# Scores of the first attention on four quarters of the array, fused sum and extreme, and the delta rule's joins as 32x32 products

## The chip, the cores and the metric

The kernel runs on one core of a Trainium2 chip. The metric is the device time of one execution in microseconds (us). The core has a matrix engine (TensorE, PE in the profile, with its weight loads as PEld), VectorE (DVE), ScalarE (ACT), GpSimd (POOL) and a queue that issues transfers (SyncE, SP). Each engine works through its own list of instructions in order; they wait for one another by semaphores.

## What is computed

Two blocks of a model on 1024 tokens of width 1024, in float32. The change touches two places.

In the first block, neighbourhood attention: 8 heads of size 64, tokens as 16 rows of 64. A row of queries sees the keys of 8 rows (512 keys), with a bias and a mask.

```python
scores = jnp.einsum('bhrnqd,bhrnikd->bhrnqik', q_blk, kg).astype(jnp.float32)
scores = jnp.where(valid[:, :, None, :], scores + bias[None], -1e30)
probs = jax.nn.softmax(scores, axis=(-2, -1)).astype(v.dtype)
out = jnp.einsum('bhrnqik,bhrnikd->bhrnqd', probs, vg)
```

In the second block, a gated delta rule in both directions over 1280 tokens in chunks of 64. Each chunk needs the inverse of a lower triangular matrix for each of 8 heads:

```python
t_mat = jnp.eye(CHUNK, dtype=jnp.float32) + bc[..., :, None] * dec_strict * kk
w_mat = lax.linalg.triangular_solve(t_mat, (bc * eG)[..., None] * kc, left_side=True, lower=True, unit_diagonal=True)
```

## The kernel before, in words

Each engine's list is written out by hand, one function for each stage and engine. PSUM's eight banks are drawn in turn by an object `bk`: `open(key)` takes the next bank, `vacant(key)` is the wait for the one who emptied it eight draws ago, `full` and `clear` are filled and emptied.

**First attention** (`tensor_natt`, `vector_natt`, `scalar_natt`, `gpsimd_natt`). The work is 64 units: unit i is one row r = i // 4 of 64 queries with a pair of heads j = i % 4. The two heads are laid out as 128 rows of a score tile of 512 keys. The queries lie in `QB` with zeros in the other head's half (cleared by two memsets, L559), so that one product of full size (contraction 128, 128 rows, 512 columns; L591) gives both heads. In PE's list iteration i holds the scores of unit i, the four transposes of unit i-3 (L600) and the eight value products of unit i-4 (L617, each on 64 columns of the array). A float32 product is two records of the profile, a transpose one. DVE adds the bias into one of two buffers `sb` (L632), takes the negated maximum (L636) and the reciprocal of the sum (L641), and splits the finished values in two (L647, L649). ACT makes the exponential with its sum (L659), then copies the transposed tile out of PSUM for unit i-3 (L667). GpSimd scales the exponentials by the reciprocal (L674) ahead of the transposes.

After the last unit the recurrent part follows (`tensor_rec`, its products under L95).

**Queries** (`vector_query_out`, L512): DVE writes each 128x512 result into `QB` in two instructions of 64 partitions.

**Delta rule** (`tensor_delta` and the others). A step takes one 128-token tile in each direction (dd = 0, 1), ten steps n. Blocks of 32x32 on the diagonal are inverted on DVE by elimination (L2241, L2244), go out to DRAM and come back in two layouts, `Y0` and `YT`; the joins then build 64x64 inverses from pairs of 32x32 ones, and 128x128 ones from those:

- join a (L2286): 16 products with a full `AT` (128x128) and `Y0` (64 columns); ACT copies four blocks of 32 partitions (L2298) into `PM`, whose other places are zero.
- join b (L2309): 16 products of full `PM` with `YT`; ACT copies four blocks back into `YT` (L2317).
- joins c, d, e (L2330, L2348, L2366): 64x64 products, with a copy by ACT after each.
- Between them stand the decay rows (L95 here) and the next key products (L2153).
- Then the step uses the inverse (L2410), DVE scales that result (L2418) in the midst of its next elimination, and so on: L2436, L2445, L2458 and L2388 on PE.

The transfers of `YT` are issued by SP (L2275), and join b waits for them (`l_yt`).

## Time and profile before

| | |
|---|---|
| Median of 3 runs | 3741.59 us (3739.25 to 3743.46) |
| The profiled execution | 3733.37 us, span 3731.6 us |
| PE busy | 3562.2 us, 95% |
| DVE, ACT, POOL busy | 1847.5, 1186.6, 704.0 us |
| Mean granted clock of TensorE | 0.981 |
| First attention, PE from its first score to the next stage | 165.1 to 322.1 us |
| Delta rule, joins a of the first and last step | 1937.7 and 2287.1 us |

Times are from the start of the span. A group of the profile gives busy time and mean length; an idle time names what ended it. Lengths of records on PE contain some 0.2 us of pipeline, so the pace of PE is read from the starts, not from the lengths.

### The profile page before, as it was taken

Reading aid. Unit: us, or ns where it says so; the run is one execution under the profiler, and the core shown is the slowest. Engines: PE = TensorE matmul, PEld = TensorE weight load, DVE = VectorE, ACT = ScalarE, POOL = GpSimd, SP = SyncE. Lnnn points to the kernel's source line nnn. Section 1 sums busy time; section 2 is a strip of 40 time slices with the busy share of each in tenths; the row PEclk is TensorE's granted clock in tenths of the full one; section 3 lists DMA queues with packets and bytes.
Section 4 is the critical chain, followed back from the end, with each engine's and each line's share of the span. In section 5 each row is a group of like instructions: output and inputs, shape, how many; then the busy total and the mean of one; then the engine's idle time right before and its main releaser. Section 6 shows DMA issues by size and latency. Waiting matters only on the chain. (4 is left out here: it accounts for less than half of the span.)

```text
span 3731.6 us, 46421 instructions
## 1 busy us (share of the span) xinstructions
PE 3562.2 (95%) x18318; PEld 2764.2 (74%) x18318; DVE 1847.5 (50%) x3351; ACT 1186.6 (32%) x2087; POOL 704.0 (19%) x532
## 2 busy tenths in 40 slices
PE   7999999999999999999988988988999999999998
PEld 6756778887888888875557877546788478888886
DVE  4276993213676555335578884669211142322322
ACT  3155772212311111234434553138211032111210
POOL 1163000010101111010020110129101113333333
PEclk9999999999999999999999998999999999999999
DMA  3100111112233232123012214000122111111111
GB/s 134 37 2 22 44 40 51 54 55 87 75 106 96 91 105 93 46 78 125 1 22 41 39 38 138 27 1 2 35 74 59 54 57 46 51 51 46 49 53 46
DMA packets 266342, 211.67 MB, mean 57 GB/s; under 512 B 65680, under 2 KB 231184, under 8 KB 265744
## 3 DMA queue, kind: packets, MB, share of 16 engines
q1 hardware_dynamic: 264368, 201.61, 17.4%
q10 hardware_dynamic: 1760, 7.08, 0.9%
q8 instruction: 149, 2.44, 0.3%
q14 instruction: 65, 0.53, 0.0%
HBM read 185.33 MB, written 21.50 MB: 55 GB/s over the span
## 5 line engine op out<-in xcount | busy, mean ns | idle before, releaser
L95 PE MATMUL ps<-halves 128*128 128x512 f32 x10408 | 2406.7, 392 | 19.1 <-DVE halves L1542 6.6
L95 PEld LDWEIGHTS ps<-halves 128*128 128x128 f32 x10408 | 1956.1, 188 | 441.4 <-issue 26.9
L95 PE MATMUL ps<-arena 128*128 128x512 f32 (+1 forms) x880 | 361.7, 564 | 11.2 <-issue 6.4
L1521 POOL TENSOR_TENSOR tmps<-tmps 128x512 f32<-128x512 f32 x128 | 143.7, 1123 | 981.4 <-ACT tmps L1489 981.4
L1542 DVE TENSOR_TENSOR halves<-tmps,halves 128x512 fp32r<-128x512 f32 x128 | 88.1, 691 | 435.4 <-ACT halves L1497 435.4
L1425 ACT ACTIVATE halves<-raws 128x2048 fp32r<-128x2048 f32 x62 | 118.3, 1909 | 556.0 <-PE ps L95 532.5
L95 PEld LDWEIGHTS ps<-arena 128*128 128x128 f32 x880 | 165.7, 193 | 170.3 <-issue 159.3
L1528 POOL TENSOR_TENSOR arena<-arena 128x512 f32<-128x512 f32 x128 | 164.8, 1294 | 191.3 <-DVE arena L1569 191.3
L1489 ACT ACTIVATE tmps<-ps 128x512 f32<-128x512 f32 x128 | 76.6, 598 | 363.9 <-PE ps L95 360.0
L1569 DVE TENSOR_TENSOR arena<-ps,arena 128x512 f32<-128x512 f32 x128 | 87.8, 690 | 194.9 <-PE ps L95 188.7
L1365 DVE SCALAR_TENSOR_TENSOR arena<-arena,sc 128x128 f32<-128x128 f32 x448 | 164.1, 366 | 15.9
L1432 DVE TENSOR_TENSOR halves<-raws,halves 128x2048 fp32r<-128x2048 f32 x62 | 142.0, 2290 | 55.3 <-ACT halves L1425 55.3
L95 PE MATMUL ps<-arena,tokens 128*128 128x512 f32 (+1 forms) x384 | 140.2, 523 | 0.0
L2943 POOL TENSOR_SCALAR arena<-arena,wst 128x640 f32<-128x640 f32 (+1 forms) x64 | 119.0, 1873 | 89.8 <-DVE wst L2897 89.7
L1559 DVE TENSOR_TENSOR arena<-arena,ps 128x512 f32<-128x512 f32 x128 | 85.2, 683 | 99.7 <-PE ps L95 99.7
L674 POOL TENSOR_SCALAR arena<-arena,sm 128x512 f32<-128x512 f32 x64 | 100.1, 1565 | 176.1 <-DVE sm L641 176.1
L2116 POOL TENSOR_TENSOR arena<-arena 128x512 f32<-128x512 f32 x40 | 44.5, 1140 | 455.0 <-PE ps L95 232.5
L1497 ACT ACTIVATE halves<-tmps 128x512 fp32r<-128x512 f32 x128 | 81.0, 633 | 154.5 <-POOL tmps L1521 154.5
L95 PEld LDWEIGHTS ps<-arena,tokens 128*128 128x128 f32 x384 | 72.4, 191 | 62.2 <-issue 59.2
L2244 DVE TENSOR_TENSOR arena<-arena 64x30 f32<-64x30 f32 (+5 forms) x300 | 103.9, 346 | 10.3
L2241 DVE TENSOR_TENSOR arena<-arena 64x30 f32<-64x30 f32 (+5 forms) x300 | 102.9, 343 | 10.0
L1093 POOL TENSOR_TENSOR valw<-valw,arena 128x512 f32<-128x512 f32 x8 | 14.0, 1748 | 444.3 <-DVE arena L1076 444.3
(306 smaller groups left out, 3532.3 us busy)
## 6 DMA issues: line engine op xcount, KB each, us to landing
raws<-in_w_ff SPq DMA_DIRECT2D x31, 1024.0 KB, 6.5
raws<-in_w_mlp SPq DMA_DIRECT2D x31, 1024.0 KB, 5.4
mixw<-in_w_in SPq DMA_DIRECT2D x56, 512.0 KB, 3.8
arena<-in_w_ada SPq DMA_DIRECT2D x48, 512.0 KB, 3.9
arena<-in_w_in SPq DMA_DIRECT2D x5, 2048.0 KB, 11.9
arena<-in_x SPq DMA_DIRECT2D x8, 1024.0 KB, 8.3
h_stash<-arena SPq DMA_DIRECT2D x1, 5120.0 KB, 30.0
inverses<-arena ACTq DMA_DIRECT2D x20, 256.0 KB, 2.9
```

What stands on the lines that cost most here:

```text
L95: ins = e.matmul(out_ap, l, r, start=i == 0, stop=i == n - 1)
L674: e.tensor_scalar(pbuf[i % 5], pbuf[i % 5], c[:, 2:3], None, ALU.mult).then_inc(*a_sl.tick())
L1365: e.scalar_tensor_tensor(out=a, in0=raw_a[:, kk, :], scalar=sc3[:, kk, b:b + 1], in1=a, op0=ALU.mult, op1=ALU.add).then_inc(*(m_part if kk ...
L1425: e.activation(RR[:, FW + q * 4096:FW + q * 4096 + 2048], raw_of(n), ACT.Copy).then_inc(*f_wh.tick())
L1432: e.tensor_tensor(RR[:, FW + q * 4096 + 2048:FW + q * 4096 + 4096], raw_of(n), RR[:, FW + q * 4096:FW + q * 4096 + 2048].bitcast(F32), ALU ...
L1521: e.tensor_tensor(tt, tt, tt, ALU.mult).then_inc(*f_sq.tick())
L1528: e.tensor_tensor(dst, dst, tmg[(i * 8 + t) % 2], ALU.add).then_inc(*f_ad.tick())
L1542: e.tensor_tensor(fl[:, m, n0:n0 + N], ftmp[x % 2], fh[:, m, n0:n0 + N].bitcast(F32), ALU.subtract).then_inc(*f_fl.tick())
L1569: e.tensor_tensor(tmg[x % 2], bk.tile(key)[:, :], G2[:, nh * 512:nh * 512 + 512], ALU.mult).then_inc(*bk.emptying(key))
L2241: e.tensor_tensor(T3, bc(W3[:, k:k + 1, k + 1:32], [64, k, 31 - k]), bc(W3[:, 0:k, k:k + 1], [64, k, 31 - k]), ALU.mult).then_inc(*dv.tick())
L2244: e.tensor_tensor(W3[:, 0:k, k + 1:32], W3[:, 0:k, k + 1:32], T3, ALU.add).then_inc(*(i_sol if k == 30 else dv).tick())
L2943: ins = e.tensor_scalar(p, p, w4[i % 4][:, 6 + s:7 + s], None, ALU.mult)
```

## The change

Three parts.

**Scores.** `QB`'s other half is no longer used and no longer cleared. A unit's two heads are two products of contraction 64 and 64 rows, each on a quarter of the array. `natt_rows(i, s)` puts head s of unit i into rows 0 to 63 or 64 to 127, exchanged in odd units; the host exchanges the bias the same way. Scores are issued for two units at once, so that four products that follow one another lie on the four quarters. Values are taken one unit later (i-5). DVE's sum and maximum become one instruction, `tensor_tensor_reduce`, which writes the negated sum and its minimum; ACT's exponential takes scale -1. The order on DVE changes, with the reciprocals in pairs.

**Queries.** One instruction of 128 partitions instead of two of 64.

**Joins a and b.** Both directions share one bank and one key. Each head's product is four 32x32 products, on four places of the array that share neither rows nor columns. `PM` and `Y0` are 256 columns, their memsets go, and ACT's four copies after join a become one of 128x256. After join b there are still four.

```diff
-            e.wait_ge(*q_zero.at(m // 2 + 1))
+            e.wait_ge(*n_xn.at(8))
             e.wait_ge(*bk.full(key))
-            for s in range(2):
-                rows = slice(64 * s, 64 * s + 64)
-                ins = e.tensor_scalar(
-                    QB[rows, m, 8 * h:8 * h + 8, s, :],
-                    bk.tile(key)[rows, :].rearrange("p (r q) -> p r q", q=64), V("bq", m)[rows], 0.125,
-                    ALU.add, ALU.mult)
-            ins.then_inc(*bk.emptying(key))
+            e.tensor_scalar(QB[:, m, 8 * h:8 * h + 8, 0, :], bk.tile(key)[:, :].rearrange("p (r q) -> p r q", q=64),
+                            V("bq", m), 0.125, ALU.add, ALU.mult).then_inc(*bk.emptying(key))
...
-            for i in range(2):
-                e.wait_ge(*n_xn.at(4 * i + 4))
-                e.memset(R(F0 + 4096 * i, 4096), 0.0).then_inc(*q_zero.tick())
...
+        def natt_rows(i, s):
+
+            a = 64 * ((s + i) % 2)
+            return slice(a, a + 64)
+
         def tensor_natt(e):
-            for i in range(64 + 4):
-                if i < 64:
-                    r, j, start = natt_place(i)
-                    key = ("as", i)
-                    o = bk.open(key, a_ev)
-                    e.wait_ge(*bk.vacant(key))
+            for i in range(64 + 5):
+                if i < 64 and i % 2 == 0:
+                    for u in (i, i + 1):
+                        bk.open(("as", u), a_es)
+                        e.wait_ge(*bk.vacant(("as", u)))
                     if i == 0:
                         e.wait_ge(*bk.clear(("q", 3, 1)))
                         e.wait_ge(*bk.clear(("k", 3, 1)))
-                    e.matmul(o[:, :], QB[:, j, r, :, :], KT[:, j, start * 64:start * 64 + 512], start=True,
-                             stop=True).then_inc(*bk.filling(key))
+                    for s in range(2):
+                        for u in (i, i + 1):
+                            r, j, start = natt_place(u)
+                            f = slice(64 * s, 64 * s + 64)
+                            ins = e.matmul(bk.tile(("as", u))[natt_rows(u, s), :], QB[f, j, r, 0, :],
+                                           KT[f, j, start * 64:start * 64 + 512], start=True, stop=True)
+                            if s == 1:
+                                ins.then_inc(*bk.filling(("as", u)))
...
-                if 0 <= i - 4 < 64:
-                    u = i - 4
+                if 0 <= i - 5 < 64:
+                    u = i - 5
...
-                                           ptb[u % 3][:, c, f], start=c == 0, stop=c == 3)
+                                           ptb[u % 3][:, c, natt_rows(u, s)], start=c == 0, stop=c == 3)
...
-                    e.tensor_tensor(sb[i % 2], bk.tile(key)[:, :], BI[:, j, off * 64:off * 64 + 512],
-                                    ALU.add).then_inc(*bk.emptying(key))
-                    c = statn[:, i % 8, :]
-                    e.wait_ge(*bk.clear(key))
-                    e.tensor_reduce(c[:, 0:1], sb[i % 2], AX.X, ALU.max, negate=True).then_inc(*a_mx.tick())
-                u = i - 1
-                if 0 <= u < 64:
-                    c = statn[:, u % 8, :]
-                    e.wait_ge(*a_ex.at(u + 1))
-                    e.reciprocal(c[:, 2:3], c[:, 1:2]).then_inc(*a_rc.tick())
-                if 0 <= i - 4 < 64:
-                    u = i - 4
-                    r, j, start = natt_place(u)
-                    key = ("ap", u)
-                    e.wait_ge(*bk.full(key))
-                    e.tensor_copy(YAH[:, j, r, :], bk.tile(key)[:, 0:64]).then_inc(*dv.tick())
-                    e.wait_ge(*dv.now())
-                    e.tensor_tensor(YAL[:, j, r, :], bk.tile(key)[:, 0:64], YAH[:, j, r, :].bitcast(F32),
-                                    ALU.subtract).then_inc(*bk.emptying(key))
+                    e.tensor_tensor_reduce(out=sb[i % 2], in0=bk.tile(key)[:, :], in1=BI[:, j, off * 64:off * 64 + 512],
+                                           scale=-1.0, scalar=3.0e38, op0=ALU.add, op1=ALU.min,
+                                           accum_out=statn[:, i % 8, 0:1]).then_inc(*bk.emptying(key))
+                for u in ((), (i - 1, i))[i % 2]:
+                    if u < 64:
+                        c = statn[:, u % 8, :]
+                        if u == i and i >= 5:
+                            vector_natt_out(e, i - 5)
+                        e.wait_ge(*a_ex.at(u + 1))
+                        e.reciprocal(c[:, 2:3], c[:, 1:2]).then_inc(*a_rc.tick())
+                if i >= 5 and (i % 2 == 0 or i >= 64):
+                    vector_natt_out(e, i - 5)
+
+        def vector_natt_out(e, u):
+            r, j, start = natt_place(u)
+            key = ("ap", u)
+            e.wait_ge(*bk.full(key))
+            e.tensor_copy(YAH[:, j, r, :], bk.tile(key)[:, 0:64]).then_inc(*dv.tick())
+            e.wait_ge(*dv.now())
+            e.tensor_tensor(YAL[:, j, r, :], bk.tile(key)[:, 0:64], YAH[:, j, r, :].bitcast(F32),
+                            ALU.subtract).then_inc(*bk.emptying(key))
...
-                    e.wait_ge(*a_mx.at(i + 1))
+                    e.wait_ge(*bk.clear(("as", i)))
                     if i >= 5:
                         e.wait_ge(*bk.full(("at", i - 5)))
-                    e.activation(pbuf[i % 5], sb[i % 2], ACT.Exp, bias=c[:, 0:1],
+                    e.activation(pbuf[i % 5], sb[i % 2], ACT.Exp, bias=c[:, 0:1], scale=-1.0,
...
-        PM = [M4(16384 + i * 1024) for i in range(2)]
-        Y0 = [R3(18432 + i * 512, 8, 64) for i in range(2)]
+        PM, Y0 = R3(16384, 8, 32), R3(18432, 8, 32)
+        QUARTERS = [(dd, q) for q in range(2) for dd in range(2)]
...
-        def tensor_join_a(e, n, dd):
-            key = ("la", n, dd)
+        def tensor_join_a(e, n):
+
+            key = ("la", n)
             o = bk.open(key, e_ea)
             e.wait_ge(*bk.vacant(key))
             e.wait_ge(*l_y0.at(4 * (n + 1)))
-            e.wait_ge(*bk.clear(("kk", n, dd, 1)))
+            for dd in range(2):
+                e.wait_ge(*bk.clear(("kk", n, dd, 1)))
             for h in range(8):
-                ins = e.matmul(o[:, h * 64:h * 64 + 64], AT[n % 2][dd][:, h, :], Y0[dd][:, h, :], start=True, stop=True)
+                for dd, q in QUARTERS:
+                    first, second = blk32(FIRST(dd, q)), blk32(SECOND(dd, q))
+                    ins = e.matmul(o[second, h * 32:h * 32 + 32], AT[n % 2][dd][first, h, second], Y0[first, h, :],
+                                   start=True, stop=True)
             ins.then_inc(*bk.filling(key))
 
-        def scalar_join_a(e, n, dd):
-            key = ("la", n, dd)
+        def scalar_join_a(e, n):
+            key = ("la", n)
             e.wait_ge(*bk.full(key))
             if n:
-                e.wait_ge(*bk.full(("lt", n - 1, dd)))
-            else:
-                e.wait_ge(*s_zero.at(3))
-            for q in range(2):
-                r = blk32(SECOND(dd, q))
-                ins = e.activation(PM[dd][r, :, blk32(FIRST(dd, q))], h8(bk.tile(key))[r, :, blk32(q)], ACT.Copy)
-            ins.then_inc(*bk.emptying(key))
-
-        def tensor_join_b(e, n, dd):
-            key = ("lt", n, dd)
+                e.wait_ge(*bk.full(("lt", n - 1)))
+            e.activation(PM, q8(bk.tile(key)), ACT.Copy).then_inc(*bk.emptying(key))
+
+        def tensor_join_b(e, n):
+            key = ("lt", n)
             o = bk.open(key, e_ea)
             e.wait_ge(*bk.vacant(key))
-            e.wait_ge(*bk.clear(("la", n, dd)))
+            e.wait_ge(*bk.clear(("la", n)))
             e.wait_ge(*l_yt.at(8 * (n + 1)))
-            y = YT[n % 2][dd].rearrange("p h (q s f) -> p h q s f", q=2, s=2)
             for h in range(8):
-                ins = e.matmul(o[:, h * 64:h * 64 + 64], PM[dd][:, h, :], y[:, h, :, 1 - dd, :], start=True, stop=True)
+                for dd, q in QUARTERS:
+                    first, second = blk32(FIRST(dd, q)), blk32(SECOND(dd, q))
+                    ins = e.matmul(o[first, h * 32:h * 32 + 32], PM[second, h, :], YT[n % 2][dd][second, h, second],
+                                   start=True, stop=True)
             ins.then_inc(*bk.filling(key))
 
-        def scalar_join_b(e, n, dd):
-            key = ("lt", n, dd)
+        def scalar_join_b(e, n):
+            key = ("lt", n)
             e.wait_ge(*bk.full(key))
-            for q in range(2):
+            for dd, q in QUARTERS:
                 r = blk32(FIRST(dd, q))
-                ins = e.activation(YT[n % 2][dd][r, :, blk32(SECOND(dd, q))], h8(bk.tile(key))[r, :, blk32(q)], ACT.Copy)
+                ins = e.activation(YT[n % 2][dd][r, :, blk32(SECOND(dd, q))], q8(bk.tile(key))[r, :, :], ACT.Copy)
...
-            for dd in range(2):
-                e.wait_ge(*bk.clear(("lt", n, dd)))
+            e.wait_ge(*bk.clear(("lt", n)))
```

On PE in the middle of the first attention, one pair of units before (psK is the bank that is written; L591 scores, L600 transposes, L617 values):

```order
L591 MATMUL ps7<-arena 128x512
L600 MATMUL ps0<-identm,arena 128x128 x4
L617 MATMUL ps1<-arena 64x64 x8
L591 MATMUL ps2<-arena 128x512
L600 MATMUL ps3<-identm,arena 128x128 x4
L617 MATMUL ps4<-arena 64x64 x8
```

and now (transposes are L602, values L619):

```order
L591 MATMUL ps6<-arena 64x512
L591 MATMUL ps7<-arena 64x512
L591 MATMUL ps6<-arena 64x512
L591 MATMUL ps7<-arena 64x512
L602 MATMUL ps0<-identm,arena 128x128 x4
L619 MATMUL ps1<-arena 64x64 x8
L602 MATMUL ps2<-identm,arena 128x128 x4
L619 MATMUL ps3<-arena 64x64 x8
```

Two products of full size have become four of a quarter each, into two banks in turn, and stand together ahead of both units' transposes and values.

On DVE in the same place, one pair of units before:

```order
L632 TENSOR_TENSOR arena<-ps,arena 128x512
L636 TENSOR_REDUCE sm<-arena 128x1
L641 RECIPROCAL sm<-sm 128x1
L647 CAST halves<-ps 128x64
L649 TENSOR_TENSOR halves<-ps,halves 128x64
L632 TENSOR_TENSOR arena<-ps,arena 128x512
L636 TENSOR_REDUCE sm<-arena 128x1
L641 RECIPROCAL sm<-sm 128x1
L647 CAST halves<-ps 128x64
L649 TENSOR_TENSOR halves<-ps,halves 128x64
```

and now:

```order
L634 ISA arena,sm<-ps,arena 128x512
L634 ISA sm 128x1
L651 CAST halves<-ps 128x64
L653 TENSOR_TENSOR halves<-ps,halves 128x64
L634 ISA arena,sm<-ps,arena 128x512
L634 ISA sm 128x1
L643 RECIPROCAL sm<-sm 128x1
L651 CAST halves<-ps 128x64
L653 TENSOR_TENSOR halves<-ps,halves 128x64
L643 RECIPROCAL sm<-sm 128x1
```

The fused instruction is two: the sum with its running minimum, and a read of the minimum. The even unit's output split now stands between the two units' sums.

On PE in the delta rule, from the end of one step through joins a, b and c, before:

```order
L2458 MATMUL ps<-arena 128x64 x8
L2286 MATMUL ps<-arena 128x64 x16
L95 MATMUL ps<-arena 128x512
L95 MATMUL ps<-halves 128x512
L2309 MATMUL ps<-arena 128x64 x16
L95 MATMUL ps<-arena 128x512
L95 MATMUL ps<-halves 128x512
L2330 MATMUL ps<-identm,arena 64x64 x16
```

and now:

```order
L2466 MATMUL ps<-arena 128x64 x8
L2297 MATMUL ps<-arena 32x32 x32
L95 MATMUL ps<-arena 128x512
L95 MATMUL ps<-halves 128x512
L2317 MATMUL ps<-arena 32x32 x32
L95 MATMUL ps<-arena 128x512
L95 MATMUL ps<-halves 128x512
L2338 MATMUL ps<-identm,arena 64x64 x16
```

Twice 16 products have become twice 32 small ones; nothing else has moved on PE.

## Rows read from the trace of the kernel before

**Rows 1.** Windows: busy (count) of PE, PEld, DVE, ACT, POOL; clock; DMA share; GB/s.

```profile
181.10:311.80 130.70, 121.97 (x1236) 76.93 (x1232) 100.49 (x281) 72.66 (x168) 87.64 (x56) 1.00 0.01 2
...
2206.40:2244.50 38.10, 32.69 (x350) 28.68 (x349) 33.60 (x83) 20.71 (x56) 4.50 (x4) 1.00 0.20 38
...
2244.50:2287.10 42.60, 34.64 (x274) 33.62 (x274) 27.50 (x75) 16.25 (x40) 2.73 (x3) 0.68 0.15 27
```

**Rows 2.** Groups by line, 181.1 to 311.8: count, busy us, mean ns.

```profile
L674 POOL TENSOR_SCALAR arena<-arena,sm 128x512 f32<-128x512 f32 x56 | 87.6, 1565 | 47.8 <-DVE sm L641 47.8
```

**Rows 3.** Timeline of the first attention: start us, us, what.

```profile
241.80 1.13 PE L591 MATMUL ps<-arena 128*128 128x512 f32 x2
...
242.77 0.60 PE L600 MATMUL ps<-identm,arena 128*128 128x128 f32 x4
...
242.97 0.69 DVE L632 TENSOR_TENSOR arena<-ps,arena 128x512 f32<-128x512 f32 x1 [0.53 <-PE ps L591]
...
243.46 0.69 PE L617 MATMUL ps<-arena 128*64 128x64 f32 x16
...
243.69 0.69 DVE L636 TENSOR_REDUCE sm<-arena 128x1 f32<-128x512 f32 x1
...
244.08 1.12 PE L591 MATMUL ps<-arena 128*128 128x512 f32 x2
...
244.41 0.72 ACT L659 ACTIVATE arena<-arena,sm 128x512 f32<-128x512 f32 x1 [1.10 <-DVE sm L636]
...
245.13 0.58 ACT L667 ACTIVATE arena<-ps 128x512 f32<-128x512 f32 x1
...
245.85 0.69 PE L617 MATMUL ps<-arena 128*64 128x64 f32 x16 [0.21 <-ACT arena L667]
...
246.47 1.13 PE L591 MATMUL ps<-arena 128*128 128x512 f32 x2
```

**Rows 4.** Timeline, PE around the first attention's start and end.

```profile
165.09 3.59 PE L591 MATMUL ps<-arena 128*128 128x512 f32 x8
...
176.80 1.06 PE L617 MATMUL ps<-arena 128*64 128x64 f32 x16 [3.29 <-DMA arena<-arena]
...
181.14 1.12 PE L591 MATMUL ps<-arena 128*128 128x512 f32 x2
...
311.80 1.12 PE L591 MATMUL ps<-arena 128*128 128x512 f32 x2
...
322.08 14.16 PE L95 MATMUL ps<-halves 128*128 128x512 f32 x61
```

**Rows 5.** Timeline, PE in the second attention.

```profile
2544.04 1.35 PE L2807 MATMUL ps<-arena 64*128 64x384 f32 x8
...
2547.16 1.31 PE L2834 MATMUL ps<-arena 128*64 128x128 f32 x20
```

**Rows 6.** Timeline of one chunk's joins, delta rule.

```profile
2131.01 3.74 PE L2286 MATMUL ps<-arena 128*128 128x64 f32 x32
...
2133.83 0.76 ACT L2298 ACTIVATE arena<-ps 32x256 f32<-32x256 f32 x2
...
2136.31 3.76 PE L2309 MATMUL ps<-arena 128*128 128x64 f32 x32 [0.42 <-DMA arena<-inverses]
...
2141.15 1.15 PE L2330 MATMUL ps<-identm,arena 64*64 64x64 f32 x32
```

**Rows 7.** Timeline, ninth chunk's step and tenth chunk's joins.

```profile
2267.84 0.69 DVE L2418 TENSOR_TENSOR arena<-ps,arena 128x512 f32<-128x512 f32 x1 [2.56 <-PE ps L2410]
...
2287.13 3.74 PE L2286 MATMUL ps<-arena 128*128 128x64 f32 x32
...
2295.39 1.15 PE L2330 MATMUL ps<-identm,arena 64*64 64x64 f32 x32 [0.94 <-ACT arena L2317]
```

**Rows 8.** Groups by line, whole span.

```profile
L822 DVE TENSOR_TENSOR_SCAN arena<-arena 128x1024 f32<-128x1024 f32 x16 | 36.7, 2291 | 0.5
```

**Rows 9.** Timeline, DVE in the program's first norm.

```profile
35.64 1.51 DVE L512 TENSOR_SCALAR arena<-ps,vec 64x512 f32<-64x512 f32 x2 [2.91 <-PE ps L95]
```

35 lines of the change are left out of this document (16 added, 19 removed).

## The prediction

> **What bounds the kernel now.** I read the page first: PE is busy for 95% of the span, and the chain that ended last runs over PE. So a change pays only where it shortens PE's list or a wait of PE. Both places of the change must be read for themselves, in windows and timelines.
>
> *First attention.* Windows show what is near its limit [rows 1]: from unit 6 at 181.1 us to unit 62 at 311.8 us, 130.7 us for 56 units, 2.33 us each, with PE busy 93%, DVE 77%, GpSimd 67%, at full clock. In the timeline [rows 3] PE's starts give the cost of a unit: scores 241.80 to 242.77, 0.97 us; transposes to 243.46, 0.69; values to 244.08, 0.62; 2.28 in all. The next score product starts 2.39 us later, after a wait of 0.21 for ACT's copy. A second thing is as long as PE's list: the way from a score product to the values that stand two units on. Scores 241.80, sum on DVE 242.97, maximum 243.69, exponential 244.41, copy 245.13, values 245.85, next but one scores 246.47: 4.67 us for two units, 2.33 each. The stage is held by this ring, and PE's own list is only 0.05 us per unit below it. Both would have to become shorter, and the change touches both.
>
> *Delta rule.* A step takes 38.1 us, of which DVE is busy 33.6 and PE 32.7 [rows 1]. DVE's eliminations set the pace; the joins run beside them. Only where DVE waits for the product L2410 behind the joins do the joins count: 2.56 us in the ninth step, and in the tenth, where no elimination is left and joins, ACT's copies and L2410 are the chain [rows 7].
>
> **Scores on quarters.** How long has a record of 512 columns the array for itself? Eight records took 3.59 us, of which the last one's length is 0.59: (3.59 - 0.59) / 7 = 0.43 us [rows 4]. Two units now cost four records, 1.94 us. In their place come eight records of a quarter. No row shows four quarters at once, but each kind of pair in the set has one: two tiles of other rows with the same columns of the array, into two banks: L2807, eight records of 384 and 256 columns, which one by one would need 4 x 0.32 + 4 x 0.21 = 2.1 us, take 1.35. Two tiles with the same rows and other columns: L2834, 20 records of 128 columns in 1.31, one by one 2.1 [rows 5]. Two tiles that share neither: L2330, 32 records of 64 columns in 1.15 us, one by one 1.7 [rows 6]. Without the pipeline's 0.2 us each of the three is two at a time. I take it that the four compose: two records after each other on each quarter, 0.86 us, and the 0.11 of overhead that 0.97 has above 0.86. With 0.1 for the change of shape ahead of the transposes, a pair of units costs 1.08 us of scores.
>
> The skill speaks against this in one place: the Trainium skill's "TensorEngine Tiling (Array Packing)", section "Restrictions and Gotchas", says that different row tiles cannot access the same PSUM bank at the same time, and here the two heads of a unit do just that. By this rule only two quarters would run together and the pair would cost 1.82 us. The trace does not agree with it for L2330, whose two tiles differ in rows and write one bank, at 0.03 us a record.
>
> **The rest of PE's pair.** Two transposes and two value groups. Upper bound: the spacings of now, 2 x (0.69 + 0.62) = 2.62; pair 3.7, with 0.13 for a wait as now 3.83. Lower bound: the 0.69 holds the wait for ACT's copy, which is gone when values are one unit later; without it the lengths less the pipeline's 0.2 us, 0.4 for four transposes (0.60) and 0.5 for 16 value records (0.69) [rows 3], with 0.1 at each change of shape, give some 2.3; pair 3.39.
>
> **DVE, ACT, GpSimd.** The sum and maximum, 0.69 each, become one instruction and a read. If it runs at the pace of the sum it is 0.69; for the read, which no row shows, I allow 0.15. The way round per pair is sum, output split, sum, exponential, reciprocal: 0.84 + 0.43 (the room between the maximum's end at 244.38 and the next sum at 245.24 holds it and the reciprocal today) + 0.84 + 0.72 and 0.25 for its own sum's read and the semaphores + 0.2 = 3.3, and 0.2 for gaps, 3.5 us. The slowest row of DVE for such work is the scan, 2291 ns for 1024 elements, 1.15 for 512 [rows 8]: that is the upper bound. GpSimd's 1.57 per unit is 3.13 per pair [rows 2]. ACT has 2 x (0.72 + 0.58) and reads, 2.7. The old ring no longer binds: the copy for unit i-3 ends 3.4 us after the pair's first score (1.2 to the sum, 0.84, 0.05, exponential 0.72, copy 0.58), and its values come a whole pair later. What is late next is then the way round on DVE and ACT, or GpSimd ahead of the transposes; both end some tenths before PE. I take 3.6 us per pair, between 3.39 and 3.83, since the way round at 3.5 lies above the lower end.
>
> **The sum of the stage.** Until the transfer for the values lands at 176.8 little can move [rows 4]; PE then has units 0 to 5 behind it instead of 0 to 4, so the pair (6, 7) starts near 177.8, against 181.14 for unit 6, and loses 0.9 to the low clock that stands there. That gives 2.4. Then 28 pairs to unit 62: 28 x (4.67 - 3.6) = 30.0. The end takes 10.3 us from unit 62's scores now, about 9.5 then (by the same working the last scaling ends 7.0 after them; transposes, copy and values follow): 0.8. Together 33.2 us; with 3.39, 39; with 3.83, 27. The next stage follows on PE without a wait [rows 4], so it all arrives at the end.
>
> **Queries.** Of two 0.75 us instructions each, one goes. Ahead of the second split of the norm stands a pair of them (1.51 us for two) [rows 9], and PE waits for that split; between nothing and 0.75 I take 0.5 us, gained once. Elsewhere PE does not wait for them: nothing. The memsets lay on GpSimd beside PE's waits for other things: nothing.
>
> **Joins.** Each takes 3.7 us on PE for 32 records of full weights [rows 6], and becomes 64 records of 32 columns on four tiles. If records follow at the 0.03 us of L2330 that is 1.9; if each tile runs at its own pace, 0.6. I take 1.4. But join b waits now for the transfer of `YT` (0.42 us, [rows 6]), so it starts when it did, and what join a gives, 2.3 us of PE and 3 of 4 copies at 0.38, is hidden behind that transfer. After join b's start: 1.4, 0.2 to ACT, four copies 1.5, 0.1 back: 3.2 us to join c, instead of 4.8 now. In the tenth step, where no wait for the transfer shows, join a starts at 2287.13; with 1.4, 0.3 to and from ACT and one copy of 0.38 join b starts near 2289.2, and join c at 2292.4 instead of 2295.39: 3.0 us. In the ninth, 2.5 of DVE's 2.56. In the other eight DVE does not wait for L2410: nothing. Sum 5.5; bounds 0 and 10 (a chain shortened by 4 to 5 us where it counts). Fewer banks drawn means older banks waited for, so no new wait there.
>
> In all 33.2 + 0.5 + 5.5 = 39.2 us. The profiled execution took 3733.37; less 39.2 is 3694.2. The median of the runs is 8.2 above the profiled one: 3702.
>
> **Rivals.**
>
> *The fused instruction runs at the scan's pace.* 1.15 + 0.19 a unit: the way round is 1.34 + 0.43 + 1.34 + 1.16 and gaps, 4.4 us a pair. For it: the scan also carries a value from element to element. Against: the maximum alone does so too and takes 0.69 [rows 3]. Gain 28 x 0.27 + 3 + 6 = 17; 3725. Chance 0.10.
>
> *Only two quarters run at a time.* A pair costs 0.86 more, 4.46; joins gain half. Gain 6 + 3 + 3 = 12; 3729. Against it stand L2330 and the pairs of rows 5; for it, that no row shows four. This is also what the rule of the tiling page would do. Chance 0.08.
>
> *The clock falls in the delta rule.* The joins leave PE idle for longer, and in the ninth step, with the clock at 0.68, a step took 42.6 instead of 38.1 us [rows 1]. If all eight others went that way: 8 x 4.5 = 36 lost of 39; 3738, no change. For it: PE waits 5.4 us in a normal step already. Against: those waits are for DVE and did not bring the clock down in the step before. Chance 0.05.
>
> *Slower: the quarters run one after another.* Eight records of 0.43 are 3.44 us; a pair 6.1, 28 x 1.4 = 40 lost at 5 gained: 3777. It decides from a cost of the four products above some 2.5 us. Against it speak all three rows of pairs. Chance 0.04.
>
> **How the numbers follow.** The forecast has 0.72, with its own range from 3690 (3.39 a pair, joins 10) to 3714 (3.83, joins 0). 0.01 is left for others. A measurement of this kernel can tell about 0.2%, 7.5 us: faster is below 3734. Faster: forecast, slow fused instruction, two at a time: 0.89. Same: the clock and remains, 0.06. Slower: 0.05. The range reaches from 3690 to the first two rivals, 3728.
>
> **What would show it.** In the profile after: scores of a pair in about 1.0 us between PE's starts, pairs 3.6 us apart from start to start; the fused instruction near 0.7 us (a wait of PE on GpSimd or of DVE on ACT says that the way round binds); the next stage starting on PE near 288.5; joins of some 1.4 us with join b still released by its transfer; steps of the delta rule still 37 to 38 us. Wrong would make it: scores of a pair at 1.8 or more, a fused instruction above 1 us, or steps above 40 us.

## The result

The changed kernel takes **3688.9 us** (median of four runs, 3687.7 to 3694.3), the kernel before beside it 3740.4: a ratio of 0.9864, 95% interval 0.9847 to 0.9881, 51 us faster. A second set of runs of both gave 0.9865 (0.9842 to 0.9889). The forecast was 3702 us, range 3690 to 3728: the direction holds and so do the two main mechanisms (quarters that run together, a broken ring), but the gain is larger than forecast, and the time is 1.1 us below the range. Two steps of the prediction failed: the time of a pair of units, 3.6 us taken for 3.42, and the delta rule's two memsets, which had no term and were worth 3.3 us.

The page of the changed kernel, profiled at 3689.1 us (the row of PEclk is TensorE's granted clock in 40 slices of the span, in tenths of full speed):

```profile
PE 3491.1 (95%) x19086; PEld 2693.1 (73%) x19086; DVE 1803.2 (49%) x3343; ACT 1175.4 (32%) x2057; POOL 693.8 (19%) x528
...
PEclk9999999999999999999988887999999999999999
```

PE's share is still 95%: its list became shorter and so did the span. The clock row has five slices below 9 in the delta rule, where before had one.

The first attention. PE's timeline in the changed kernel at two places, the start and the steady part:

```profile
177.91 1.99 PE L591 MATMUL ps<-arena 64*64 64x512 f32 x8
...
182.50 1.09 PE L591 MATMUL ps<-arena 64*64 64x512 f32 x8
```

```profile
247.53 1.09 PE L591 MATMUL ps<-arena 64*64 64x512 f32 x8
248.56 0.65 PE L602 MATMUL ps<-identm,arena 128*128 128x128 f32 x4
249.14 0.69 PE L619 MATMUL ps<-arena 128*64 128x64 f32 x16
...
250.96 1.09 PE L591 MATMUL ps<-arena 64*64 64x512 f32 x8
```

Against [rows 3, 4]: eight records of scores for two units take 1.02 us from start to start (247.53 to 248.56) where two units took 1.94; transposes follow at 0.58 and values at 0.61 to 0.62; no row of PE shows a wait; a pair takes 3.42 us (ten pairs from 240.69 to 274.92) where two units took 4.67. The other engines over those ten pairs, grouped by line with shapes apart (count, busy us, mean ns, idle before):

```profile
L678 POOL TENSOR_SCALAR arena<-arena,sm 128x512 f32<-128x512 f32 x20 | 31.1, 1567 | 3.2 <-DVE sm L643 3.2
...
L634 DVE CUSTOM_DVE_ANT_0 arena<-ps,arena 128x512 f32<-128x512 f32 x20 | 13.7, 686 | 1.1 <-PE ps L602 0.2
...
L634 DVE DVE_READ_ACCUMULATOR2_ANT sm<- 128x1 f32 x21 | 1.7, 82 | 0.0
```

The fused instruction takes 0.69 us and its read 0.08. GpSimd is idle for 3.2 of 34.2 us, less than DVE and ACT are; that it is next in line p9 shows below.

The end of the stage and the delta rule, PE's timeline at three places:

```profile
283.88 1.43 PE L95 MATMUL ps<-halves 128*128 128x512 f32 x5
```

```profile
1885.97 1.10 PE L95 MATMUL ps<-arena 128*128 128x512 f32 x2 [3.36 <-issue]
...
1896.53 0.75 PE L2297 MATMUL ps<-arena 32*32 32x32 f32 x64
```

```profile
2240.44 0.75 PE L2297 MATMUL ps<-arena 32*32 32x32 f32 x64
2243.29 0.74 PE L2317 MATMUL ps<-arena 32*32 32x32 f32 x64 [2.10 <-DMA arena<-inverses]
2245.76 1.97 PE L2338 MATMUL ps<-identm,arena 64*64 64x64 f32 x32 [1.72 <-ACT arena L2326]
2248.51 1.98 PE L2356 MATMUL ps<-arena 64*64 64x64 f32 x32 [0.78 <-ACT arena L2346]
...
2254.61 7.06 PE L2418 MATMUL ps<-arena 128*128 128x64 f32 x32 [1.38 <-ACT arena L2382]
```

The next stage starts on PE at 283.88 where it was 322.08 [rows 4]: 38.2 us. The first join a starts at 1896.53 where it was 1937.84: 41.3. In the tenth step join a takes 0.75 us and join b 0.74 where each took 3.7, but joins c to e take 1.97 us where the profile of before shows 1.15 [rows 6, 7].

### The profile page after: what moved, and what is told of

Read it like the earlier page. It is cut to its first block and busy times, and to the rows that moved or that the text cites. A ratio compares the mean times of both kernels' runs of the same rounds, so it can differ in the third digit from the quotient of the medians.

```text
span 3687.3 us, 47926 instructions
## 1 busy us (share of the span) xinstructions
PE 3491.1 (95%) x19086; PEld 2693.1 (73%) x19086; DVE 1803.2 (49%) x3343; ACT 1175.4 (32%) x2057; POOL 693.8 (19%) x528
## 5 line engine op out<-in xcount | busy, mean ns | idle before, releaser
L95 PEld LDWEIGHTS ps<-arena 128*128 128x128 f32 x880 | 165.2, 193 | 167.3 <-issue 156.2
L2123 POOL TENSOR_TENSOR arena<-arena 128x512 f32<-128x512 f32 x40 | 44.5, 1141 | 451.5 <-PE ps L95 232.7
L2251 DVE TENSOR_TENSOR arena<-arena 64x30 f32<-64x30 f32 (+5 forms) x300 | 102.3, 341 | 10.3
```

The source lines that it names most:

```text
L95: ins = e.matmul(out_ap, l, r, start=i == 0, stop=i == n - 1)
L2251: e.tensor_tensor(W3[:, 0:k, k + 1:32], W3[:, 0:k, k + 1:32], T3, ALU.add).then_inc(*(i_sol if k == 30 else dv).tick())
```

## The experiments

Fourteen runs, two of them the kernel before and the changed one again. A table first of what their profiles show in the delta rule, read from starts in PE's timelines. *Ahead*: from PE's first product for the decays (L2079 of before), which opens the delta rule's own work on PE, to the first join a. *Rule*: from the first join a to the first product of the second attention (L2684 of before). Profiled executions are single ones, so only differences that come again count.

| kernel | median us | profiled us | ahead | rule |
|---|---|---|---|---|
| before | 3740.4 | 3733.4 | 68.0 | 408.9 |
| b2_before_again | 3743.7 | 3744.8 | 68.7 | 415.7 |
| p1_attention_only (old joins) | 3704.4 | 3703.2 | 68.0 | 418.2 |
| p6_quarters_only (old joins) | 3742.6 | 3735.1 | 68.4 | 409.6 |
| p7_values_later_only (old joins) | 3724.6 | 3724.6 | 68.7 | 415.6 |
| after | 3688.9 | 3689.1 | 64.7 | 405.2 |
| a2_after_again | 3690.7 | 3689.8 | 64.8 | 407.9 |
| p2_joins_only | 3732.6 | 3732.9 | 64.8 | 408.1 |
| p3_memsets_back | 3693.6 | 3692.9 | 68.0 | 406.6 |
| p4, p5, p8, p9 (new joins, no memsets) | below | | 66.2, 64.8, 64.8, 64.8 | 407.3, 408.1, 405.6, 406.5 |
| v1_memset_later | 3693.9 | 3694.2 | 68.1 | 405.2 |
| v2_kept_busy | 3690.0 | 3690.4 | 68.2 | 402.1 |
| v3_kept_busy_late | 3683.5 | 3686.9 | 64.8 | 400.4 |

### The parts apart

**p1_attention_only**: the new attention and queries, the delta rule of before.

```diff
-                    tensor_join_a(e, n)
+                    for dd in BOTH:
+                        tensor_join_a(e, n, dd)
...
+            e.memset(R(16384, 2048), 0.0).then_inc(*s_zero.tick())
+            e.memset(R(18432, 1024), 0.0).then_inc(*s_zero.tick())
```

> Attention and queries as in the changed kernel, delta rule as before (joins of full size, two memsets kept). Main theory: the attention's gain is carried whole to the end, 38.2 us of the trace, so 3740.4 - 38.2 = 3702. Rival, the joins and memsets carry more than the 6 us that the trace shows between (44.2 in all): this kernel would then lie above 3706. Rival, the profiled execution of the kernel before was a fast one and the whole change is worth 51.5: part of the missing 7 us shows here, 3697 or below.

Measured 3704.4 us, ratio 0.990 (0.9887 to 0.9914), 38.6 below the 3742.9 of the kernel before, run beside it. This is the main theory's number (3702) within the runs' scatter. The attention is worth 38.6 by runs and 38.2 by the trace.

**p2_joins_only**: the reverse.

```diff
-                    for dd in BOTH:
-                        tensor_join_a(e, n, dd)
+                    tensor_join_a(e, n)
...
-            e.memset(R(16384, 2048), 0.0).then_inc(*s_zero.tick())
-            e.memset(R(18432, 1024), 0.0).then_inc(*s_zero.tick())
```

> Kernel before with the delta rule of the changed one (32x32 joins, memsets gone), attention untouched. Main theory: 3.3 us by the memsets and 3 by the joins, 3734. Rival, joins as forecast and no memset term: 5.5, 3735, told from the first by the step at the first join a in the trace (earlier by 3.3 or by nothing). Rival, the lower clock that idle joins bring eats all: 3740.

Measured 3732.6 us, ratio 0.9972 (0.9962 to 0.9981): 10.3 us below the kernel before, run beside it, where the main theory said 6.3. Both parts together give 48.9, the change 51 with an interval of 6 either way: no remainder can be told. But the two traces of before and after differ by 44.2 us only. So either the parts hide something or the profile of before was not typical of its runs.

**b2_before_again**: the kernel before, unchanged, to see that.

> The kernel before once more, for a second profile. First theory: the profiled execution of before (3733.4, 9 us below the median of its runs) had a rare good passage through the delta rule; a typical one shows one step there some 7 to 8 us longer (the first, 37.1 us in that profile, 44.9 in the kernel with the new attention alone), and a span near 3740. Rival: the executions differ by small amounts everywhere, and no stage holds the 9 us.

The profile came out at 3744.8 us. The first step took 40.6 us from join c to join c, not 44.9, so the 7 to 8 us in one step are refuted; but 6.8 of the 11.4 us between the two profiles lie in the delta rule (table), and 4.8 of them behind the tenth join c. PE's timeline there in the second profile, joins c and d, where the first profile has 1.15 us for join c [rows 7]:

```profile
2300.80 1.88 PE L2330 MATMUL ps<-identm,arena 64*64 64x64 f32 x32 [0.94 <-ACT arena L2317]
2303.45 1.98 PE L2348 MATMUL ps<-arena 64*64 64x64 f32 x32 [0.78 <-ACT arena L2338]
```

Windows of both profiles, the first and then the second, over the time in which DVE waits for that product (columns as in [rows 1]):

```profile
2288.10:2304.00 15.90, 12.02 (x171) 11.59 (x170) 0.06 (x1) 5.38 (x12) 1.30 (x2) 0.98 0.58 201
```

```profile
2293.60:2313.00 19.40, 15.52 (x168) 14.94 (x168) 0.02 (x1) 5.38 (x12) 2.00 (x2) 0.69 0.50 166
```

The same products ran at a clock of 0.98 in one execution and of 0.69 in the other: 1.15 or 1.88 to 1.98 us a join. In the five profiles with the old joins DVE's waits for the product behind them sum to 23.9, 28.2, 25.9, 22.8 and 28.2 us; with the new joins (after, a2, p2, p3, p4) to 21.1, 21.2, 22.2, 22.0 and 20.7. The profile of before was one of two in five (p6 is the other) in which the tenth step ran at the higher clock: from join c to the next stage 51.4 us in these two, 56.2 in the other three, and 54.9 to 56.3 in all eight profiles with the new joins. By the table the rule takes 413.6 us on average over the five profiles with the old joins and 406.9 over the eight with the new ones: 6.7 us.

**p3_memsets_back**: the change with the two memsets of the delta rule put back.

```diff
             e.memset(R(12288, 4096), 0.0).then_inc(*s_zero.tick())
+            e.memset(R(16384, 2048), 0.0).then_inc(*s_zero.tick())
+            e.memset(R(18432, 1024), 0.0).then_inc(*s_zero.tick())
             gpsimd_gates(e, 1, 1)
```

> Changed kernel with the two memsets of the delta rule back at their place on GpSimd and the waits for them. Main theory: GpSimd comes 3.3 us later to the gates that the decay rows wait for, and it arrives at the end: 3688.9 + 3.3 = 3692.2, decay rows' wait on PE back from 3.4 to some 6.5 us. Rival, the 3.3 us come from the joins or from the attention's new end, and the memsets are hidden: 3689.

Measured 3693.6 us, ratio 0.987 (0.9855 to 0.9885), against 0.9864 for the change: by the runs alone 2 us with an interval of some 5 on each, not told from nothing. The traces tell it: GpSimd's timeline with the memsets back,

```profile
1881.52 1.80 POOL L2628 MEMSET arena<- 128x2048 f32 x1
...
1884.19 3.45 POOL L2123 TENSOR_TENSOR arena<-arena 128x512 f32<-128x512 f32 x2
```

PE's wait for the decay rows there,

```profile
1887.73 2.05 PE L95 MATMUL ps<-arena 128*128 128x512 f32 x2 [6.00 <-issue]
```

and a distance ahead of the first join a of 68.0 us. In the kernel before, the same rows on GpSimd and PE are

```profile
1920.53 1.80 POOL L2622 MEMSET arena<- 128x2048 f32 x1
1922.28 1.49 POOL L2623 MEMSET arena<- 128x1024 f32 x1
1923.74 3.35 POOL L2116 TENSOR_TENSOR arena<-arena 128x512 f32<-128x512 f32 x2
```

```profile
1927.18 2.04 PE L95 MATMUL ps<-arena 128*128 128x512 f32 x2 [6.44 <-issue]
```

All six profiles with the memsets have 68.0 to 68.7; of the eight without them and with GpSimd's order untouched seven have 64.7 to 64.9, and p4 66.2. The gates (L2123, L2116 of before) start right behind the memsets, PE waits 6.00 us for them in place of 3.36, and the distance is 3.3 us longer. The wait is 2.6 of these; the other 0.65 is the step's first product, 2.60 us from its start to join a's at a granted clock of 0.73, in place of 1.95 at 1.00. (p4's 66.2 is the same: that product took 3.40 us there, at a clock of 0.56.) These 3.3 us are a term that I had set at nothing.

### What in the attention gave the gain

**p6_quarters_only**: the kernel before with a unit's two heads on two quarters.

```diff
-                    e.matmul(o[:, :], QB[:, j, r, :, :], KT[:, j, start * 64:start * 64 + 512], start=True,
-                             stop=True).then_inc(*bk.filling(key))
+                    for s in range(2):
+                        f = slice(64 * s, 64 * s + 64)
+                        ins = e.matmul(o[f, :], QB[f, j, r, s, :], KT[f, j, start * 64:start * 64 + 512],
+                                       start=True, stop=True)
+                    ins.then_inc(*bk.filling(key))
```

> Kernel before with each unit's score product as two quarters (64 rows by 64 columns each, other rows and other columns of the array, one bank), all else as before. Main theory: the two run together, 0.97 becomes 0.55 us; the ring of 4.67 us over two units holds one such product, so 0.4 per two units, 28 x 0.4 + 1 = 12 to 13 us: 3730. Rival, by the rule that two row tiles can't write one bank at a time (the Trainium skill, TensorEngine Tiling (Array Packing), Restrictions and Gotchas): they run one after another, 0.97 us, 3743.

Measured 3742.6 us, ratio 0.9999 (0.9986 to 1.0013). Both expectations had the arithmetic wrong, and the trace sets it right:

```profile
242.54 1.08 PE L593 MATMUL ps<-arena 64*64 64x512 f32 x4
243.55 0.66 PE L603 MATMUL ps<-identm,arena 128*128 128x128 f32 x4
...
247.17 1.08 PE L593 MATMUL ps<-arena 64*64 64x512 f32 x4
```

Four records of 512 columns start 1.01 us before the transposes; one after another they would need 4 x 0.43 = 1.7. So the two quarters do run together, in one bank and with different rows. Serial they would have cost 64 x 0.7 = 45 us, and nothing was lost. The Trainium skill (TensorEngine Tiling (Array Packing), Restrictions and Gotchas) says that different row tiles can't access one bank at the same time; this trace does not agree for tiles that write different partitions of the bank, as these do. No run here has two row tiles on the same partitions of one bank. But two quarters with 512 columns each take as long here (1.01 us) as the product of full size (0.97), so a unit alone gains nothing by them. Only when four are filled, two units at a time, is anything saved.

**p8_unit_by_unit**: the change with the four products in another order.

```diff
-                    for s in range(2):
-                        for u in (i, i + 1):
+                    for u in (i, i + 1):
+                        for s in range(2):
```

> Changed kernel with the pair's four score products issued unit by unit (both heads of one unit, then both of the next) in place of head by head. Main theory: what counts is that the four stand on four quarters, whatever their order; the exchanged rows of odd units keep it so, and the scores of a pair still take 1.0 us: 3689. Rival, products share the array only with their direct neighbours: two and two, 1.9 us a pair as two full products: 31 x 0.9 = 28 more, 3716.

Measured 3691.7 us, ratio 0.9861 (0.9845 to 0.9878), and in PE's timeline a pair of 3.43 us (246.01 to 249.44) with scores of 1.02 (to 247.03). Head by head or unit by unit makes no difference.

**p4_full_scores**: the change with full-size products for the scores.

```diff
-                    for s in range(2):
-                        for u in (i, i + 1):
-                            r, j, start = natt_place(u)
-                            f = slice(64 * s, 64 * s + 64)
-                            ins = e.matmul(bk.tile(("as", u))[natt_rows(u, s), :], QB[f, j, r, 0, :],
-                                           KT[f, j, start * 64:start * 64 + 512], start=True, stop=True)
...
+                    for u in (i, i + 1):
+                        r, j, start = natt_place(u)
+                        e.matmul(bk.tile(("as", u))[:, :], QB[:, j, r, :, :],
+                                 KT[:, j, start * 64:start * 64 + 512], start=True,
+                                 stop=True).then_inc(*bk.filling(("as", u)))
```

> Changed kernel with scores as one full-size product per unit again (queries padded with zeros, two instructions and memsets for that as before); pairs, values one unit later and the fused instruction stay. Main theory: PE's list is the bound, a pair costs 0.92 us more (1.94 for 1.02): 4.34 us a pair, 31 x 0.92 = 29 us more, and 0 to 0.8 for the queries: 3718. Rival, most of the gain is the broken ring and the shorter way round, quarters matter little: 3695 or below.

Measured 3714.5 us, ratio 0.9927 (0.9915 to 0.994): 25.6 us more than the change by medians, 24 by ratios. A pair:

```profile
283.56 1.99 PE L597 MATMUL ps<-arena 128*128 128x512 f32 x4
285.38 0.60 PE L607 MATMUL ps<-identm,arena 128*128 128x128 f32 x4
...
287.73 0.70 PE L597 MATMUL ps<-arena 128*128 128x512 f32 x1
```

4.17 us, 0.75 more than with quarters. Scores cost 0.80 more (1.82 for 1.02; back to back two full products are cheaper than twice 0.97), and the first transposes behind them 0.05 less.

**p7_values_later_only**: the kernel before with values at i-5 in place of i-4, on PE and DVE.

```diff
-            for i in range(64 + 4):
+            for i in range(64 + 5):
...
-                if 0 <= i - 4 < 64:
-                    u = i - 4
+                if 0 <= i - 5 < 64:
+                    u = i - 5
```

> Kernel before with values one unit later (i-5 on PE and DVE), all else as before: the ring over two units is cut. Main theory: PE's own list binds, 2.28 us less the transposes' wait, near 2.2 a unit: 60 x 0.1 = 6 us, 3736. Rival, most of the change's gain is this edit: below 3725. Rival, DVE's splits now wait in front of the sums and nothing comes: 3742.

Measured 3724.6 us, ratio 0.9947 (0.9934 to 0.996): 17 us by medians (20 by ratios, and 17.3 by the start of the next stage, 304.73 for 322.08), three times my theory's 6. The ring is cut and PE's list binds, but that list is shorter than I had read it:

```profile
227.08 1.12 PE L591 MATMUL ps<-arena 128*128 128x512 f32 x2
228.04 0.60 PE L600 MATMUL ps<-identm,arena 128*128 128x128 f32 x4
228.57 0.69 PE L617 MATMUL ps<-arena 128*64 128x64 f32 x16
229.19 0.70 PE L591 MATMUL ps<-arena 128*128 128x512 f32 x1
```

2.11 us a unit: transposes to values 0.53, not 0.69. The difference is the wait of the values for ACT's copy, which is gone here, and which no row of PE had shown as a wait.

**p5_two_instructions**: the change with sum and negated maximum apart again.

```diff
-                    e.tensor_tensor_reduce(out=sb[i % 2], in0=bk.tile(key)[:, :], in1=BI[:, j, off * 64:off * 64 + 512],
-                                           scale=-1.0, scalar=3.0e38, op0=ALU.add, op1=ALU.min,
-                                           accum_out=statn[:, i % 8, 0:1]).then_inc(*bk.emptying(key))
+                    e.tensor_tensor(sb[i % 2], bk.tile(key)[:, :], BI[:, j, off * 64:off * 64 + 512],
+                                    ALU.add).then_inc(*bk.emptying(key))
+                    c = statn[:, i % 8, :]
+                    e.wait_ge(*bk.clear(key))
+                    e.tensor_reduce(c[:, 0:1], sb[i % 2], AX.X, ALU.max, negate=True).then_inc(*a_mx.tick())
```

> Changed kernel with sum and negated maximum as two instructions on DVE (0.69 us each) in place of the fused one; order, pairs, quarters and values stay. Main theory: the way round over DVE and ACT, 3.3 to 3.4 us a pair now, becomes 2 x 0.65 longer, 4.6 to 4.7, and binds: 30 pairs x 1.2 = 36 us, 3725. Rival, DVE has room (it is busy for half of the stage) and PE's list still binds: 3689.

Measured 3711.7 us, ratio 0.9912 (0.9899 to 0.9925): 23 us more than the change by medians, 18 by ratios, and less than the 36 expected. A pair is 4.08 us (score starts 277.75 and 281.83), and PE waits inside it for GpSimd, which waits for DVE's reciprocals; DVE's only wait from one even unit's sum (277.38) to the next (281.46) is for ACT's exponential:

```profile
278.94 3.11 POOL L680 TENSOR_SCALAR arena<-arena,sm 128x512 f32<-128x512 f32 x2 [0.97 <-DVE sm L645]
...
279.66 0.17 DVE L645 RECIPROCAL sm<-sm 128x1 f32<-128x1 f32 x1 [0.43 <-ACT arena L665]
...
280.65 0.63 PE L602 MATMUL ps<-identm,arena 128*128 128x128 f32 x4 [0.62 <-POOL arena L680]
```

So the way round over DVE and ACT does bind here, as expected, but at 4.08 and not 4.6 to 4.7 us: the 3.3 to 3.4 from which I started held a wait of DVE for PE. The way itself, without the two maxima, is some 2.8 us.

**p9_half_values** leaves out two of the four value products of each head, so that PE's list is shorter.

```diff
-                    for c in range(4):
+                    for c in range(2):
```

> Changed kernel with two of the four value products of each head left out in the first attention, so PE's list is some 0.25 us shorter per unit and nothing else changes. If PE's list alone sets the pair's 3.42 us, the pair falls until the next limit. GpSimd at 2 x 1.57 us is 3.13, the way round over DVE and ACT by the starts of the trace some 3.2: a pair of 3.15 to 3.25, 30 x 0.2 = 6 us less, 3683. Rival, the way round that the forecast put at 3.5 is the limit already: 3.42 stays, 3689. Rival, nothing but PE counts: 2.95, 14 us less, 3675.

Measured 3677.8 us, ratio 0.9829 (0.9805 to 0.9852), 13 us less than the change, run beside it. The timeline of all engines, GpSimd's scaling and PE's scores:

```profile
239.60 7.73 POOL L678 TENSOR_SCALAR arena<-arena,sm 128x512 f32<-128x512 f32 x5
...
240.71 0.21 PEld L591 LDWEIGHTS ps<-arena 64*64 64x64 f32 x8
...
243.79 0.21 PEld L591 LDWEIGHTS ps<-arena 64*64 64x64 f32 x8
```

A pair is 3.08 us, a little below the 3.15 to 3.25 expected, and GpSimd has no gap left: five scalings in 7.73 us, 3.09 for two. So PE's list alone set 3.42, the way round over DVE and ACT, which I had put at 3.5, is at most 3.1, and the next limit is GpSimd. (Thirty pairs of 0.34 us are 10 of the 13 us; where the other 3 lie is not shown.)

### Two further edits, and a version that is faster than both

**v1_memset_later**: the change with GpSimd's remaining memset behind the last gates.

```diff
-            e.memset(R(12288, 4096), 0.0).then_inc(*s_zero.tick())
             gpsimd_gates(e, 1, 1)
+            e.memset(R(12288, 4096), 0.0).then_inc(*s_zero.tick())
```

> Changed kernel with GpSimd's remaining 3.5 us memset at the delta rule's start put behind the last gates in place of ahead of them. Main theory: as with the two memsets that the change took away, the decay rows on PE come earlier by what stood in front of the gates, 3.4 us, and it arrives at the end: ratio to the kernel before lower by 0.0009 than that of the changed kernel, some 3685 to 3686. Rival, the next thing ready at that place (DVE's or ACT's work on the inputs) is late by itself and nothing comes: 3689.

Measured 3693.9 us, ratio 0.9865 (0.9848 to 0.9882): nothing. The decay rows are on time, as wanted, and PE waits behind them instead, for DVE:

```profile
1893.77 2.37 PE L1871 MATMUL ps<-identm,arena 128*128 128x128 f32 x10 [6.07 <-DVE arena L1969]
1897.88 3.76 PE L2396 MATMUL ps<-arena 128*128 128x128 f32 x16 [1.74 <-POOL arena L2630]
```

The distance ahead is back to 68.1 us. Of the 3.4 us that are lost against the change, 0.8 is DVE, which comes later to what the transposes L1871 wait for; the way from these to the first product L2396 takes 4.1 us for 3.3 and that product 3.7 for 1.95 (starts 1893.77, 1897.88 and join a's 1901.56), 2.6 together. PE stood idle for 6.07 us just before, and the granted clock of this stretch was 0.62, in the changed kernel 0.84:

```profile
1889.00:1901.60 12.60, 6.09 (x30) 5.52 (x32) 7.23 (x11) 6.55 (x19) 4.86 (x6) 0.62 0.29 53
```

```profile
1886.00:1896.50 10.50, 8.29 (x48) 5.69 (x48) 6.88 (x11) 6.27 (x19) 3.05 (x5) 0.84 0.30 55
```

**v2_kept_busy**: v1, and products without use where PE waits, from the eighth step on.

```diff
+        def keep_busy(e, n, o, k, w=512):
+            if n >= FROM:
+                for _ in range(k):
+                    e.matmul(o[:, 0:w], ident[:, :], kT[:, 0, 0:w], start=True, stop=True)
...
+            keep_busy(e, n, o, 2 if n < 9 else 1)
             e.wait_ge(*bk.clear(("la", n)))
...
+            keep_busy(e, n, o, 3 - 3 * dd)
             if n:
                 e.wait_ge(*e_st.at(turn[n - 1, dd] + 1))
```

> The one with the later memset, and in the last three steps of the delta rule products without use (128x512 or 128x256, into a bank that the next product overwrites) where PE waits: three ahead of the step's first product, two or one ahead of join b, one ahead of joins c, d, e and of the product behind them. Theory of the clock: the tenth step's chain runs at a granted clock of 0.62 because PE waits so much; kept busy it runs near 0.98, the joins c to e take 1.15 in place of 1.97 us and the product behind them 3.76 in place of 7.06: 5 us less than the one with the later memset alone, 3681. Rival, the extra products stand in the way as much as the clock gives: no difference. Rival, the clock does not come back: 2 to 4 us more.

Measured 3690.0 us, ratio 0.9849 (0.9831 to 0.9867): 3.8 us less than v1, run beside it, where 5 were expected from a theory that had v1 at 3686. The clock did come back: joins d and e of the tenth step take 1.15 us, the product behind them 3.76, and the way from the tenth join c to the next stage 48.8 in place of 56.0 us. But the eighth and ninth distance from join c to join c are 41.4 and 38.9 us, for 38.1 and 37.7: the three products ahead of the step's first stand in its way, and DVE waits up to 6.2 us for it.

**v3_kept_busy_late**: the same on the changed kernel, in the last two steps and where the waits are longer than the products.

```diff
+            if n >= 8:
...
+            keep_busy(e, n, o, 2 if (n, dd) == (9, 0) else 0)
             if n:
                 e.wait_ge(*e_st.at(turn[n - 1, dd] + 1))
```

> Changed kernel (memset where it was), with products without use only in the last two steps and only where the trace shows PE waiting longer than they take: two or one ahead of join b, one ahead of joins c, d, e and of the product behind them, two ahead of the tenth step's first. Theory of the clock: the steps before stay at 37 to 38 us (they were 41.4 and 38.9 with three products ahead of each step's first), the tenth step's way from join c to the next stage is 49 instead of 56 us: 6 us less than the changed kernel, 3683. Rival, the clock needs the earlier steps kept busy too: no gain, 3689.

Measured **3683.5 us** (3679.6 to 3686.9), ratio 0.9842 (0.9821 to 0.9863); the changed kernel, run beside it, had 3690.7 (3689.8 to 3693.6), so 7.2 us less, and its slowest run is below the other's fastest: the fastest version that computes all. PE's timeline in the tenth step (L2393 are the products without use):

```profile
2251.84 1.97 PE L2359 MATMUL ps<-arena 64*64 64x64 f32 x32
2253.74 1.15 PE L2393 MATMUL ps<-arena,identm 128*128 128x256 f32 x2
2254.82 1.15 PE L2378 MATMUL ps<-arena 64*64 64x64 f32 x32
...
2257.35 0.85 PE L2429 MATMUL ps<-arena 128*128 128x64 f32 x6 [0.33 <-ACT arena L2386]
```

Join e and the product behind it run at the higher level again; joins c and d still at the lower. Windows of the changed kernel and of this one, over the tenth step's joins and that product (columns as in [rows 1]):

```profile
2240.40:2262.00 21.60, 14.85 (x260) 14.17 (x259) 2.01 (x4) 4.86 (x10) 2.49 (x2) 0.62 0.47 155
```

```profile
2242.80:2264.00 21.20, 18.71 (x294) 14.45 (x294) 2.49 (x5) 6.94 (x17) 2.49 (x2) 0.84 0.54 173
```

The way from the tenth join c to the next stage is 50.3 us for 56.0 (49 expected). The one from the eighth to the ninth is 40.2, where 37 to 38 were expected; a2 and p9, which have no such products, show 39.6 there, so it is not told from scatter. The rule takes 400.4 us by the trace, 5 to 8 less than in the two profiles of the change.

**a2_after_again**: the changed kernel once more.

> The changed kernel once more, for a second profile and a ratio with more runs: 0.9864 of the kernel before, 3689 to 3692. In the delta rule the tenth step's wait of DVE for the product behind the joins is again near 17 us, and the first join a stands 64.5 us behind the last product of the stage ahead, if the 3.3 us at the start of the delta rule are no accident of one execution.

Measured 3690.7 us, ratio 0.9865 (0.9842 to 0.9889); 64.8 us ahead, and the table's last column 407.9. The start of the delta rule came again to a tenth, and DVE's wait in the tenth step (16.88 us, before 16.87) as well.

## Why the prediction missed, point by point

**Reading what bounds the kernel.** Right for the attention: it was a ring of 4.67 us, PE's list next to it. Wrong in how near: I read PE's list as 2.28 us a unit, and cut from the ring (p7) it is 2.11. That reading counted a wait inside PE's groups as work. The lower end of the pair's time, further down in the same text, did take this wait out; the reading of the bound and p7's expectation did not use it.

**Scores on quarters.** 1.08 us forecast, 1.02 measured, and the pair that the row of L2330 stood for (other rows and columns, one bank) holds (p6). Stacked as the runs stack them, for two units: 4.67 us; 4.63 with quarters alone (p6, 242.54 to 247.17); 4.21 with the ring cut alone (p7); 4.17 with ring cut, pairs and fused instruction (p4); 4.08 with all but the fused instruction (p5); 3.42 with all. Quarters alone give nothing and the cut ring alone less than half, since each bound stands just behind the other. The fused instruction alone was not run; taking it away from the whole costs 18 to 23 us, taking the quarters away 24 to 26.

**The pair, 3.6 us taken, 3.42 measured: the step that failed first.** I had 3.39 as the lower end for PE's list, which was right, and set it aside because I put the way round at 3.5. That sum was too long: p9 ran a pair in 3.08, with GpSimd as the limit, and there the way round itself, with DVE's wait for PE left out, is 0.70 from the first sum to the output split, 0.40 to the second sum, 0.72 to the exponential, 0.85 to the reciprocal and 0.15 to the next sum: 2.8 us. With two maxima more it is the 4.08 of p5. The 0.7 us too many were small allowances at every link (0.84, 0.43, 0.84, 0.97 and 0.2 were taken), and 0.2 for gaps on top. The bound was PE's list, as the lower end had it. The stage gave, by its starts, 3.2 at the beginning (2.4 forecast; the pair (6, 7) at 177.91, forecast 177.8), 33.7 over the 28 pairs to the last one's start at 274.92 (30.0 forecast; the first of them took 4.59 at the low clock), 1.3 at the end (0.8 forecast): 38.2 for 33.2. With 3.42 in place of 3.6 the forecast's own sum, 2.4 + 28 x (4.67 - 3.42) + 0.8, gives 38.2 as well, so this one term accounts for the miss of the stage; the 0.8 and 0.5 us more at its start and end are about what its slow first pair cost.

**Queries, 0.5 us forecast: not to be told.** The first score product starts at 165.3 us, before 165.1; over the sixteen profiles it starts between 163.0 and 167.3 whatever the kernel, so no run shows a term of 0.5 or its absence.

**Memsets, costed at nothing: 3.3 us, the step that was plainly wrong.** I looked at the two memsets of the queries and never wrote down what stood behind the two in the delta rule on GpSimd's queue: the gates, for which PE's decay rows waited. The row was there to be read in the trace of before (a wait of 6.44 us on PE). p3 brought it back. This is also what puts the result outside the range: its lower end is a pair of 3.39 and joins worth 10, which by the text's own terms is 39 + 0.5 + 10 = 49.5 us and 3692 (the text has 3690), and with 3.3 more it would have been 3689.

**Joins, 5.5 us forecast, 6.7 measured.** The two sizes agree within what the profiles scatter, but that is partly luck, for the terms do not. In the tenth step join a to join c is 5.32 us (2240.44 to 2245.76), forecast 5.3, before 8.3, and by another way: joins of 0.75 us instead of my 1.4, and join b now waits 2.10 us for its transfer, where I had it free. Little of these 3.0 us arrives: DVE's waits for the tenth step's two products behind the joins are 19.7 us on average in the five profiles named above, with the old joins 20.8, so 1.1 less, because joins c to e and the product behind them run at the lower clock in all eight profiles with the new joins and in three of five with the old. In the ninth step these waits fall from 4.3 to 1.7 us, 2.6 for the 2.5 forecast. With 0.6 in earlier steps DVE waits 4.3 us less; where the other 2 to 3 lie in the steps is not told apart by these runs. Join b waits for its transfer in all ten steps, as forecast for nine (34.1 us in all, before 5.1).

**The profile against the median.** I set the sum against a profile of 3733.4 and added 8.2 for the median (3741.6; the runs beside the changed kernel gave 3740.4). This cost the forecast 1.2 us, but that profile's tenth step was at a clock of 0.98, which only two of five executions with the old joins came near, so the two traces alone show 44 us where the runs show 51. In sum: 38.6 for the attention, 3.3 and 6.7 in the delta rule make 48.6, against 39.2 forecast; the remaining 3 of the 51.5 us are inside the scatter.

**Rivals.** The fused instruction at the scan's pace: refuted (0.69 + 0.08). Two quarters at a time: refuted by 1.02 us and by p8 (the prediction prices it twice, 1.82 for 1.08 us of scores and 0.86 more a pair; neither was seen). Quarters serial: refuted. The clock falling in the delta rule: it does, for part: the window of the whole rule has 0.84 in the changed kernel; joins c at 1.97 us in most steps. It costs nothing in the steps before the ninth join c, which take 300.4 us together in the changed kernel and 300.6 before (DVE sets their pace), but it does in the tenth, where v3 took most of its 7 us back. It was a rival for 36 us, and is worth some 7, of which the old joins paid a part too.
